# Decode attention turns of a one-core hybrid layer: value products directly behind the scores, the output row's copy first, and the projection of the last four turns divided

## The reference

```python
ls = jnp.einsum('btkgd,bktnld->bktgnl', q, kg).astype(f32) * scale + bias_s
ps = masked_softmax(ls, (dist_s >= 0)[:, :, :, None], (-2, -1))
o_s = jnp.einsum('bktgnl,bktnld->btkgd', ps, vg.astype(f32))
...
lw = jnp.einsum('btkgd,bskd->bkgts', q, kw).astype(f32) * scale + bias_w
pw = masked_softmax(lw, mask_w, -1)
o_w = jnp.einsum('bkgts,bskd->btkgd', pw, vw.astype(f32))
...
y = jnp.sum(gate[..., None] * o * jax.nn.silu(z.astype(jnp.float32)), axis=2)
y = y.reshape(b, t, Q_WIDTH).astype(x.dtype)
return x + rms_norm(y @ w_out, g_post)
```

## Time and profile before

| | |
|---|---|
| median of 3 runs | 888.9 us (887.4 to 890.23) |
| the profiled execution, its own time | 890.47 us |
| its span, first to last instruction | 888.7 us |
| TensorE clock, mean granted | 0.999 |
| PE busy | 861.2 us (97%) |
| DVE busy | 559.0 us (63%) |
| ACT busy | 452.6 us (51%) |
| start of turn 4 to start of turn 15 (key transposes, L2446) | 806.81 to 856.13 us |

### The profile page before, as it was taken

The page is one execution under the profiler, slowest core; times in us unless marked ns, Lnnn a source line. Parts: engine busy times, 40 slices in busy tenths (PEclk is TensorE's granted clock), DMA queues, the critical chain, the costliest instruction groups (busy, mean ns, idle before and its releaser), DMA issues.

```text
span 888.7 us, 16698 instructions
## 1 busy us (share of the span) xinstructions
PE 861.2 (97%) x6202; PEld 756.7 (85%) x6202; DVE 559.0 (63%) x1211; ACT 452.6 (51%) x916; POOL 300.4 (34%) x311
## 2 busy tenths in 40 slices
PE   5999999999999999999999999999999999999996
PEld 4999999955888778889999999999999998786664
DVE  6379999998967683333245565656564655536563
ACT  6466777643742543234256565646565655424231
POOL 2389888879050000003013232323233233400000
PEclk9999999999999999999999999999999999999999
DMA  9456343217249465057224142332332003913521
GB/s 244 106 133 191 97 120 80 63 43 242 66 163 367 179 231 151 21 134 221 73 49 91 33 93 48 73 68 60 66 73 48 25 1 82 281 57 117 171 85 36
DMA packets 158165, 99.52 MB, mean 112 GB/s; under 512 B 97202, under 2 KB 147026, under 8 KB 158005
## 3 DMA queue, kind: packets, MB, share of 16 engines
q1 hardware_dynamic: 143278, 79.30, 33.6%
q0 software_dynamic: 4896, 10.32, 3.2%
q10 hardware_dynamic: 9911, 8.84, 3.0%
HBM read 89.58 MB, written 18.85 MB: 122 GB/s over the span
## 4 chain that ended last, share of the span: by engine, by line
PE 91%; DVE 4%; issue 2%; ACT 2%; ACTq 1%; POOL 1%; DVEq 0%; POOLq 0%
PE psum L2312 7%; PE psum L2311 7%; PE psum L2313 7%; PE psum L1960 6%; PE psum L1961 6%; PE psum L1962 6%; PE psum L2409 6%; PE psum L2038 5%; PE psum L2151 5%; PE psum L2152 4%; PE psum L2153 4%; PE psum L2360 4%; PE psum L2377 4%; PE psum L2342 4%; PE psum L1941 2%; PE psum L2483 2%
## 5 line engine op out<-in xcount | busy, mean ns | idle before, releaser
L822 ACT ACTIVATE arena<-psum 128x512 f32<-128x512 f32 (+9 forms) x227 | 90.2, 434 | 162.3 <-PE psum L2313 74.7
L2311 PE MATMUL psum<-u_hi,tile_hi 128*128 128x288 f32 x464 | 142.0, 306 | 1.0 <-issue 1.0
L801 POOL TENSOR_SCALAR arena<-arena,kept 128x512 f32<-128x512 f32 (+3 forms) x128 | 82.8, 661 | 163.8 <-DVE kept L1797 163.8
L2312 PE MATMUL psum<-u_lo,tile_hi 128*128 128x288 f32 x464 | 137.4, 296 | 0.0
L2313 PE MATMUL psum<-u_hi,tile_lo 128*128 128x288 f32 x464 | 136.3, 294 | 0.0
L1447 DVE SCALAR_TENSOR_TENSOR psum<-arena,psum 128x512 f32<-128x512 f32 x168 | 127.0, 756 | 6.0
L1960 PE MATMUL psum<-h_hi,tile_hi 128*128 128x288 f32 x352 | 104.5, 297 | 0.0
L1961 PE MATMUL psum<-h_lo,tile_hi 128*128 128x288 f32 x352 | 104.3, 296 | 0.0
L1962 PE MATMUL psum<-h_hi,tile_lo 128*128 128x288 f32 x352 | 104.0, 295 | 0.0
L1274 ACT ACTIVATE arena<-arena,kept 128x512 f32<-128x512 f32 (+3 forms) x128 | 70.4, 551 | 40.1 <-DVE kept L1763 40.1
L2311 PEld LDWEIGHTS psum<-u_hi,tile_hi 128*128 128x128 f32 x464 | 87.4, 188 | 1.4 <-issue 1.2
(11 more groups left out here) (328 smaller groups left out, 1880.1 us busy)
## 6 DMA issues: line engine op xcount, KB each, us to landing
tile_whole<-in_b_w_in SPq DMA_DIRECT2D x64, 256.0 KB
tile_whole<-in_a_w_in SPq DMA_DIRECT2D x24, 512.0 KB
arena<-in_cmp_w SPq DMA_DIRECT2D x4, 2048.0 KB, 9.7
kvw_whole<-in_w_kv SPq DMA_DIRECT2D x6, 1024.0 KB, 14.2
bias_copies<-bias_line POOLq DMA_DIRECT2D x4, 1280.0 KB, 23.5
arena<-in_x_prompt SPq DMA_DIRECT2D x8, 512.0 KB, 6.8
kvw_whole<-in_a_w_out SPq DMA_DIRECT2D x4, 1024.0 KB, 11.3
arena<-bias_copies SPq DMA_DIRECT2D x16, 256.0 KB, 3.8
```

What stands on the lines that cost most here:

```text
L801: pool.tensor_scalar(L, L, rden[:, stat(n) + k:stat(n) + k + 1], gR[:, i, h:h + 1], ALU.mult, ALU.mult).then_inc(S["pn_ready"], 1)
L822: return nc.scalar.activation(out, in_, ACT.Copy, scale=scale)
L2311: pe.matmul(pb(b, HT), w_hi, u_hi[:, k, here], start=(k == 0), stop=False)
L2312: pe.matmul(pb(b, HT), w_hi, u_lo[:, k, here], start=False, stop=False)
```

## The change

Three edits, in the turns alone. On DVE the copy of the output row (L1907) moves ahead of the two copies of probabilities (L1900, L1901). On PE the values move from the end of the turn to directly behind the scores, so that the transposes of the probabilities end the turn. In the last four turns (16 to 19), which have no key transposes, the half of the projection is cut in up to three pieces: one ahead of the output row's transpose, one ahead of the values, one at the turn's end, with 2, 2, 0 steps in turns 16 and 17, 2, 1, 1 in turn 18, and 1, 3, 0 in turn 19.

```diff
--- before.py
+++ after.py
@@ -1890,6 +1890,12 @@
                     k = 8 + n % 4
                     V.tensor_tensor_reduce(l_sb[:, 1 + n % 3, 0:KS], pb(1, KS), bs, 1.0, 3 * BIG, ALU.add, ALU.min,
                                            mn[:, k:k + 1]).then_inc(S["sl_ready"], 1)
+                n = w - 3
+                if 0 <= n < 2 * DB:
+                    dve.wait_ge(S["so_mm"], n + 2)
+                    if n >= 2:
+                        dve.wait_ge(S["ot_tr"], n)
+                    V.tensor_copy(orow[:, n % 2], pb(3, P)).then_inc(S["or_ready"], 1)
                 n = w - 2
                 if 0 <= n < 2 * DB:
                     dve.wait_ge(S["st_tr"], n + 2)
@@ -1899,12 +1905,6 @@
                         dve.wait_ge(S["pv_done"], N_ITEMS)
                     V.tensor_copy(pts[:, n % 2, 0:2], pb(2, 2, P)).then_inc(S["pts_ready"], 1)
                     V.tensor_copy(pts[0:DS, n % 2, 2], pb(2, 3, P, p1=DS)[:, 2]).then_inc(S["pts_ready"], 1)
-                n = w - 3
-                if 0 <= n < 2 * DB:
-                    dve.wait_ge(S["so_mm"], n + 2)
-                    if n >= 2:
-                        dve.wait_ge(S["ot_tr"], n)
-                    V.tensor_copy(orow[:, n % 2], pb(3, P)).then_inc(S["or_ready"], 1)
                 if w in norm_at and norm_at[w] < 3:
                     last_mean(norm_at[w])
                 if w - 1 in norm_at and norm_at[w - 1] < 3:
@@ -2435,6 +2435,7 @@
                 ins = pe.transpose(pb(2, DB, P)[:, b], orc[:, b], ident)
             ins.then_inc(S["ot_tr"], 1)
 
+            LATE_CUTS = ((2, 4), (2, 4), (2, 3), (1, 4))
             for w in range(2 * DB + 4):
                 n = w
                 if n < 2 * DB:
@@ -2445,11 +2446,15 @@
                         for pg in range(2):
                             ins = pe.transpose(pb(0, 2, 2, P)[:, p, pg], cache_sb[n % 6][:, pg, p * P:(p + 1) * P], ident)
                     ins.then_inc(S["skt_tr"], 1)
+                if w >= 2 * DB:
+                    h = halves_at[w][0]
+                    cut = [4 * (h % 2) + k for k in (0,) + LATE_CUTS[w - 2 * DB] + (4,)]
+                    last_part(4 + h // 2, range(cut[0], cut[1]))
                 n = w - 4
                 if 0 <= n < 2 * DB:
                     pe.wait_ge(S["or_ready"], 1 + (n + 1))
                     pe.transpose(pb(3, P), orow[:, n % 2], ident).then_inc(S["ot_tr"], 1)
-                for h in halves_at.get(w, ()):
+                for h in halves_at.get(w, ()) if w < 2 * DB else ():
                     last_part(4 + h // 2, range(4 * (h % 2), 4 * (h % 2) + 4))
                 n = w - 1
                 if 0 <= n < 2 * DB:
@@ -2460,6 +2465,19 @@
                         ins = pe.matmul(pb(1, KS, p0=64 * p, p1=64 * p + 64), qbd[:, n // 2, p], kts[:, n % 2, p],
                                         start=True, stop=True)
                     ins.then_inc(S["ss_mm"], 1)
+                if w >= 2 * DB:
+                    last_part(4 + h // 2, range(cut[1], cut[2]))
+                n = w - 3
+                if 0 <= n < 2 * DB:
+                    pe.wait_ge(S["pts_ready"], 1 + 2 * (n + 1))
+                    pe.wait_ge(S["ys_mul"], 2 * DB + 2 * n)
+                    for j in range(3):
+                        for p in range(2):
+                            rows_p, cols_p = slice(64 * p, 64 * p + 64), slice(P * p, P * p + P)
+                            weights = pts[:, n % 2, j, rows_p] if j < 2 else pts[0:DS, n % 2, 2, rows_p]
+                            held = cache_sb[n % 6][:, j, CH:2 * CH][:, cols_p] if j < 2 else vnew[:, n % 6, cols_p]
+                            ins = pe.matmul(pb(3, P, p0=64 * p, p1=64 * p + 64), weights, held, start=(j == 0), stop=(j == 2))
+                    ins.then_inc(S["so_mm"], 1)
                 n = w - 2
                 if 0 <= n < 2 * DB:
                     pe.wait_ge(S["sp_ready"], n + 2)
@@ -2471,17 +2489,8 @@
                         k = min(P, KS - j * P)
                         ins = pe.transpose(pb(2, 3, P, p1=k)[:, j], l_sb[:, 1 + n % 3, j * P:j * P + k], ident)
                     ins.then_inc(S["st_tr"], 1)
-                n = w - 3
-                if 0 <= n < 2 * DB:
-                    pe.wait_ge(S["pts_ready"], 1 + 2 * (n + 1))
-                    pe.wait_ge(S["ys_mul"], 2 * DB + 2 * n)
-                    for j in range(3):
-                        for p in range(2):
-                            rows_p, cols_p = slice(64 * p, 64 * p + 64), slice(P * p, P * p + P)
-                            weights = pts[:, n % 2, j, rows_p] if j < 2 else pts[0:DS, n % 2, 2, rows_p]
-                            held = cache_sb[n % 6][:, j, CH:2 * CH][:, cols_p] if j < 2 else vnew[:, n % 6, cols_p]
-                            ins = pe.matmul(pb(3, P, p0=64 * p, p1=64 * p + 64), weights, held, start=(j == 0), stop=(j == 2))
-                    ins.then_inc(S["so_mm"], 1)
+                if w >= 2 * DB:
+                    last_part(4 + h // 2, range(cut[2], cut[3]))
 
             pe.wait_ge(S["y_s"], 2)
             pe.wait_ge(S["fy"], 3)
```

## The result

The changed kernel takes 883.88 us (median of 8 runs, 882.03 to 885.12) against 888.8 us (8 runs, 887.12 to 890.23): ratio 0.9944, 95% interval 0.993 to 0.9957, some 5 us or 0.6% faster. The forecast was 883.9 us, 5.0 us faster. The profiled execution took 883.54 us with a span of 881.7.

A forecast was written before the change was run, and what follows sets the result against it. PE, busy 97% of the span, was taken as the bound. 3.9 us from thirteen ordinary turns plus 1.1 from the last four make 5.0, from the median 888.9 to 883.9 us; range 882.8 to 887.4.

The forecast's parts named there:

- The ordinary turns: Turns 3 to 15 on PE: five changes of weight shape become three, 4.48 to 4.18 us each, 3.9 us.
- entry: Start of a PE group whose weight shape differs from the group before: 0.07 us of the 0.15 remainder.
- The nearest row for what no row showed: L2377 ahead of L2419, both 128x64 weights: no exit seen, so scores next to values were taken to save 0.15 us.
- Rival 1: Ordinary turns: only one of the two neighbourhoods pays, 0.15 us a turn, 3.0 us in all, 885.9 us; chance 0.16.
- Rival 2: Ordinary turns: the 0.15 belongs to groups and their waits, turns stay 4.48, only the end gains, 887.8 us; chance 0.15.
- Rival 3: Ordinary turns: DVE's in-order queue becomes the bound and delays the gating, 2.8 us slower, 891.7 us; chance 0.04.
- the margin: Turns with the scaling behind them: the gating on DVE ends 0.26 us ahead of PE's start of the values.
- the 0.39 stall: PE's wait for L1907 ahead of the output row's transpose, at each of the last four turns before the change.
- The last four turns: Turns 16 to 19: 13.33 us against 14.41, a gain of 1.1 us.
- the stall for the gating: Turn 18: PE could start the values at 1.55 but the gating is done at 1.71, a new stall of 0.16 us.
- the last wait: PE's wait ahead of L2491, for DVE's adds, grows from 0.29 to some 0.9 us.

The follow-up runs named there:

- e1: Changed kernel with the projection halves of turns 16 to 19 whole, in their old place behind the output row's transpose: 883.63 us, ratio 0.9947.
- e5: Changed kernel with the values' second part (8x64 weights) ahead of the first (128x64), nothing else changed: 885.46 us, ratio 0.9959.
- e6: Changed kernel with the values' second part padded from 8 rows to 128 by zeros, so all twelve instructions load 128x64 weights: 881.06 us, ratio 0.9899.
- e4: Changed kernel with DVE's old order, the two probability copies ahead of the output row's copy: 892.52 us, ratio 1.0039.

## Why the prediction held

- *The ordinary turns.* Forecast 4.18 and 3.9 us over thirteen turns, measured 4.15 and 4.26. Each group had its length as forecast within 0.02 (scores 0.49 for 0.51, first part 0.54 for 0.52, second 0.36, probability transposes 0.39, key transposes 0.43) but the row transpose, 0.11 for 0.14. That term of the sum was too large. I had carried over 0.14 from the earlier trace rows without asking why a transpose of 128 columns took longer than the 0.107 of the four ahead of it. In the kernel before it comes 0.08 behind the end of the row's copy, at the very edge of its release, so the 0.03 look like the rest of that wait; in the kernel after the copy is done long before. A row transpose that plainly waited, as in e1 (865.96 to 866.12), has its successor 0.16 behind it, which fits. This reading was argued from the rows and not tried by itself. Turn 3, the first of the thirteen, gains less than the others (0.24, from 6.01 to 5.77): in the kernel before no values stand ahead of that turn's key transposes, so they had no entry to save.
- *The nearest row for what no row showed.* That scores and values as neighbours save 0.15 was taken from two other groups with 128x64 weights. Rival 1 (3.0 us in all) asked less of it, and so did the rule of the Trainium skill ("TensorE: Matmul & The Clock Gate", Part 3) that a weight load overlaps running matmuls only where the row group differs (4.1 in all). Here the trace differs from that rule: the values' first loads, with all 128 rows, start 0.22 ahead of the first product while the scores, with the same rows, still run, and the measurement decides. e5 put the 0.15 back by the order of the products alone. The prediction called every difference of shape a change; by its own count it left out the 128x8 transpose, and it came out right because that one costs nothing.
- *Rival 2,* remainders that belong to groups, fell with the 4.15 and with e5 and e6.
- *Rival 3,* DVE's queue as the bound: the margin was worked out as 0.26 and measured as 0.29, without a wait of PE in any ordinary turn. But e4 shows how near its other side was: with the copies in the old order the turn is 4.83. The prediction priced the new order's dangers and named the 0.39 stall as what comes if the cover is gone; it did not say that DVE's edit carries the change, at 9 us.
- *The last four turns.* Forecast 13.33, measured 13.39, with the stall for the gating at 0.22 (0.16) and the last wait at 0.77 (0.9). The prediction priced the new order and the division together and never the undivided halves. The sum was right, but the division is no ground for it: e1 has 13.1 undivided. The new place of the values brings the gain, and the division takes 0.3 back, by a change of shape in turn 16, the gating in turn 18 and a last row transpose that comes a step later than it could.
- *The total.* 5.0 forecast, 4.9 by the medians and 5.3 by the stage. That the median came out at 883.88 for 883.9 is closer than the method is; runs of one kernel spread by 3 us.

## What to carry to other kernels

Count, in PE's timeline, how often neighbouring groups differ in the shape of their weights, rows as well as columns (a transpose with fewer columns of weights cost nothing here). A change between 128x128, 128x64 and 8x64 costs 0.15 us here though the engine shows as busy throughout, so put groups of one shape side by side, and pad a small one to its neighbour's shape if that adds no columns. When a group moves on one engine, look at what else stands in the queue of the engine that answers it: the copy that PE needs first has to be first there too, and what is queued behind a moved step is part of its price.

## What the runs showed beyond that

- A transpose with 128x8 or 128x60 weights among 128x128 ones shows no cost of its own, where 8x64, 60x128 and 128x64 do.
- Padding the weights from 8 rows to 128 made a group faster, 0.76 us in place of 0.90, with the same columns streamed.
- The stage has the same length in two executions of the changed kernel (82.43 and 82.43 us), while the start of the stage lies anywhere from 783.9 to 787.5 us in the twelve traces, whose instructions up to there are the same but for two memsets on POOL in three of them. The two executions of the changed kernel are 1.0 us apart in total and 1.0 in the start of the stage, so all of that difference comes from ahead of it. An effect of 0.4 us is clear in a stage's length and lost in a median.
